# Row maxima read two banks at a time from one pair buffer, in a four-layer attention kernel

## What is computed

```python
def mla_attend(q_nope, q_rope, k_nope, k_rope, v):
    def attend(qn, qr):
        s = (jnp.einsum('bqhd,bkhd->bhqk', qn, k_nope) + jnp.einsum('bqhr,bkr->bhqk', qr, k_rope)) * scale
        p = jax.nn.softmax(s, axis=-1)
        return jnp.einsum('bhqk,bkhd->bqhd', p.astype(v.dtype), v)
...
def gqa_dense(q, k, v, sink=None):
    def attend(qb):
        s = jnp.einsum('bqhgd,bkhd->bhgqk', qb, k) * scale
        p = jax.nn.softmax(s, axis=-1)
        return jnp.einsum('bhgqk,bkhd->bqhgd', p.astype(v.dtype), v)
```

## Time and profile before

| | |
|---|---|
| median of 3 runs | 3619.41 us (3611.78 to 3621.05) |
| the profiled execution | 3618.99 us, its span 3617.2 us |
| PE, DVE, ACT, POOL busy | 3456.4, 2400.3, 2155.9, 1272.3 us |
| granted TensorE clock, mean | 0.989 |
| attention stretches (first to last p_f) | 401 to 925 (MLA), 1337 to 1804 (GQA), 2199 to 2524 (SWA), 2984 to 3493 us (MLA) |

### The profile page before, as it was taken

The page is one execution under the profiler, slowest core; times in us unless marked ns, Lnnn a source line. Parts: engine busy times, 40 slices in busy tenths (PEclk is TensorE's granted clock), DMA queues, the critical chain, the costliest instruction groups (busy, mean ns, idle before and its releaser), DMA issues. The chain is left out here.

```text
span 3617.2 us, 82216 instructions
## 1 busy us (share of the span) xinstructions
PE 3456.4 (96%) x33644; PEld 2060.7 (57%) x33644; DVE 2400.3 (66%) x3920; ACT 2155.9 (60%) x2859; POOL 1272.3 (35%) x1315
## 2 busy tenths in 40 slices
PE   6999999999999989999999998999999999999998
PEld 3554566666555556666645556666455446666654
DVE  6426688888466639999846517887553458888854
ACT  5424687887434438888823226887343338888861
POOL 0000255555230016666612003666120005555542
PEclk9999999999999999999999999999999999999999
DMA  6127523332112443333111335442112482222211
GB/s 256 52 86 218 158 69 78 82 82 65 68 36 59 130 122 74 82 75 74 43 73 52 96 115 131 109 113 69 69 46 69 134 224 56 56 56 60 53 50 59
DMA packets 373333, 325.50 MB, mean 90 GB/s; under 512 B 246272, under 2 KB 294080, under 8 KB 371424
## 3 DMA queue, kind: packets, MB, share of 16 engines
q1 hardware_dynamic: 372960, 320.24, 32.5%
HBM read 228.94 MB, written 91.23 MB: 89 GB/s over the span
## 5 line engine op out<-in xcount | busy, mean ns | idle before, releaser
L2421 POOL TENSOR_TENSOR p_lo<-p_f,p_hi 128x512 f16<-128x512 f32 (+2 forms) x768 | 836.3, 1089 | 725.2 <-DVE p_lo L2357 402.2
L2233 PE MATMUL bank<-q_slots,k_slots 96*128 96x512 f16 (+7 forms) x3968 | 1047.0, 365 | 30.3 <-PEq L1436 16.2
L798 PE MATMUL bank<-H_hilo,w_hilo 128*128 128x512 f16 (+1 forms) x5760 | 1044.7, 344 | 13.9 <-DVE w_hilo L1048 9.3
L2052 DVE TENSOR_REDUCE max_parts<-bank 128x1 f32<-128x512 f32 (+2 forms) x1536 | 959.9, 646 | 111.0 <-PE bank L1996 97.1
L2309 ACT ACTIVATE p_f<-bank 128x1024 f32<-128x1024 f32 (+2 forms) x768 | 743.5, 968 | 260.5 <-PE bank L2233 246.4
L798 PEld LDWEIGHTS bank<-H_hilo,w_hilo 128*128 128x128 f16 x5760 | 563.4, 98 | 495.0 <-DVE w_hilo L1048 10.3
L2316 ACT ACTIVATE p_hi<-bank 128x1024 f16<-128x1024 f32 (+2 forms) x768 | 743.6, 968 | 0.0
L2357 DVE TENSOR_TENSOR p_lo<-p_f,p_hi 128x512 f16<-128x512 f32 (+2 forms) x768 | 578.6, 753 | 155.4 <-ACT p_hi L2316 149.2
L1996 PE MATMUL bank<-k_slots,q_slots 96*128 96x512 f16 (+4 forms) x1536 | 561.8, 368 | 23.4 <-DVE max_parts L2052 13.1
L2233 PEld LDWEIGHTS bank<-q_slots,k_slots 96*128 96x128 f16 (+2 forms) x3968 | 345.0, 98 | 294.1 <-issue 49.4
L1012 ACT ACTIVATE z_ring<-bank 128x512 f32<-128x512 f32 (+1 forms) x192 | 87.5, 528 | 429.4 <-PE bank L798 416.1
(11 more groups left out here) (205 smaller groups left out, 4004.0 us busy)
## 6 DMA issues: line engine op xcount, KB each, us to landing
ada_w<-in_w_ada SPq DMA_DIRECT2D x48, 768.0 KB, 6.4
gate<-z_ring SPq DMA_DIRECT2D x32, 640.0 KB, 3.3
gate_rows<-gate SPq DMA_DIRECT2D x32, 640.0 KB, 4.0
q_slots<-q_mla SPq DMA_DIRECT2D x64, 240.0 KB, 3.3
k_mla<-H_hilo SPq DMA_DIRECT2D x64, 224.0 KB, 3.2
k_slots<-k_mla SPq DMA_DIRECT2D x64, 224.0 KB, 4.6
cq_hilo<-v_scratch SPq DMA_DIRECT2D x64, 224.0 KB, 4.2
v_lo_hi_one<-v_scratch SPq DMA_DIRECT2D x64, 224.0 KB, 4.2
```

The lines of the kernel that those rows point to most:

```text
L798: ins = pe.matmul(dst, lhs(a, k), rhs(b, k), start=(k == 0 and n == 0), stop=(k == nk - 1 and n == 2))
L2052: found = dve.tensor_reduce(mx[:, o, t, c:c + 1], mb[:, 0:nk], AX.X, ALU.max)
L2233: scored = pe.matmul(dst, lhs, rhs, start=(m == 0), stop=(m == len(ops) - 1), skip_group_check=swa)
L2421: pool.tensor_tensor(pl[:, g % 4, cols // 2:cols], p32[:, g % 3, cols // 2:cols], ph[:, g % 4, cols // 2:cols], ALU.subtract).then_inc(s_p ...
```

## The change

Two neighbouring entries of maxima become one: PE writes them into the two halves of bank pair 2, one DVE instruction reduces both (in MLA and GQA to two columns of `mx`; in SWA, where a pair is the two parts of one query tile, 896 or 768 columns to one). There is one such pair buffer. All other entries (turn, out, ada) share one bank, half of bank pair 3. `wait_bank` waits for the entry before of the same kind, paired or not. The lists give one pair per step. Both products of a pair stand behind the first score block, `ada` behind the last, `out` behind PV; DVE takes the pair first, `ada` and `out` last. The core of the diff:

```diff
-        SB, MB = [bank[0], bank[1]], [bank[2][:, 0], bank[2][:, 1], bank[3][:, 1]]
+        SB, MB = [bank[0], bank[1]], [bank[2][:, 0], bank[2][:, 1]]
         OB = bank[3][:, 0]
-        R = len(MB)
+        PAIR, ONE = bank[2], bank[3][:, 1]
...
+            return [("max", u, n // 2, blocks[n:n + 2]) for n in range(0, len(blocks), 2)]
...
-        out_step = [{4: 1, 5: 2}, {8: 0}] if swa else [{5: 1, 6: 2}, {11: 0}]
+        out_step = [{5: 1, 6: 2}, {8: 0}] if swa else [{7: 1, 8: 2}, {11: 0}]
...
         if swa:
-            own = [b_[5:7] + c_[:1], b_[7:] + c_[1:], [turn(1)], [turn(2)], [], [], [], [], []]
-            ahead = [[], [], [], a_[:2], a_[2:4], a_[4:6], a_[6:] + b_[:1], b_[1:3] + mod, [turn(0)] + b_[3:5]]
+            own = [b_[1:2], b_[2:3], b_[3:4], [turn(1)] + c_, [turn(2)], [], [], [], []]
+            ahead = [[]] * 4 + [a_[0:1], a_[1:2], a_[2:3], a_[3:4] + mod, [turn(0)] + b_[0:1]]
         else:
-            own = [b_[6:9], b_[9:11] + c_[:1], b_[11:] + c_[1:], [turn(1)], [turn(2)]] + [[]] * 8
-            ahead = [[]] * 4 + [a_[:2], a_[2:4], a_[4:6], a_[6:8], a_[8:10], a_[10:], b_[:3], mod + b_[3:4],
-                                [turn(0)] + b_[4:6]]
+            own = [b_[1:2], b_[2:3], b_[3:4], b_[4:5], b_[5:6], [turn(1)] + c_, [turn(2)]] + [[]] * 6
+            ahead = [[]] * 6 + [a_[0:1], a_[1:2], a_[2:3], a_[3:4], a_[4:5] + mod, a_[5:6], [turn(0)] + b_[0:1]]
...
+            if stream[b][n][1][0] == "max":
+                return PAIR
+            return MB[0] if isinstance(i, int) and i < 0 else ONE
...
-            m = place[b, n]
+            m = ring.index((b, n))
+            paired = stream[b][n][1][0] == "max"
             while True:
-                m -= R
+                m -= 1
...
-                if ring[m] is not None and wait_taken(pe, i, *ring[m]):
+                kb, kn = ring[m]
+                if (stream[kb][kn][1][0] == "max") == paired and wait_taken(pe, i, kb, kn):
                     return
...
-            found = dve.tensor_reduce(mx[:, o, t, c:c + 1], mb[:, 0:nk], AX.X, ALU.max)
+            nk = blocks[1][2]
+            if swa and u < 2:
+                found = dve.tensor_reduce(mx[:, o, n2:n2 + 1], mb[:].rearrange("p b n -> p (b n)")[:, 0:PAST + nk],
+                                          AX.X, ALU.max)
+            else:
+                found = dve.tensor_reduce(mx[:, o, 2 * n2:2 * n2 + 2], mb[:, :, 0:nk], AX.X, ALU.max)
```

More of the change, by code:

```diff
@@ L1747, in maxima_of @@
             q0, nq = units[u]
-            found = []
-            for t in range(nq // P):
-                if u == 2:
-                    found.append(("max", u, t, 0, PAST + LAT, CTX, []))
-                elif not swa:
-                    found += [("max", u, t, c, c * 512, 512, []) for c in range(3)]
-                else:
+            tiles = range(nq // P)
+            if u == 2:
+                blocks = [(t, PAST + LAT, CTX, []) for t in tiles]
+            elif not swa:
+                blocks = [(t, c * 512, 512, []) for t in tiles for c in range(3)]
+            else:
+                blocks = []
+                for t in tiles:
                     i = q0 // P + t
@@ L1809, in entry_bank, with of_kind @@
         def entry_bank(i, b, n):
-            if isinstance(i, int) and i < 0:
-                return MB[sum(d for d, e in stream[b][:n]) % 2]
-            return MB[place[b, n] % R]
+            if stream[b][n][1][0] == "max":
+                return PAIR
+            return MB[0] if isinstance(i, int) and i < 0 else ONE
+        def of_kind(b, found, *kinds):
+            return [n for n in found if stream[b][n][1][0] in kinds]
         P2 = 2 * NS
@@ L1905, in wait_bank @@
                 earlier = [m for m in range(n) if stream[b][m][0] == 1]
-                for m in earlier[-2::-2]:
+                for m in earlier[::-1]:
                     if wait_taken(pe, i, b, m):
@@ L2043, in take_entry @@
                 return
-            _, u, t, c, k0, nk, masks = e
+            _, u, n2, blocks = e
             o = turn_order[u]
@@ L2107, in attention @@
         before = [n for n, (d, e) in enumerate(stream[1]) if d == 1]
-        at_tile = [3, 3, 4, 5, 5, 6, 7, 7, 8, 8, 9, 9, 10, 10, 10, 10, 10] if swa else [3 + k * 2 // 5 for k in range(NE)]
+        at_tile = [4, 5, 6, 7, 7, 9, 10] if swa else [3, 4, 5, 6, 7, 7, 8, 9, 10] if ada else [3, 4, 5, 6, 7, 8, 9, 10]
         make_values(dict(n=len(before), at_tile=lambda k: at_tile[k], load_v=lambda sp: load_v(sp, 0, 0, 0),
@@ L2240, in body @@
                                 if n == 0:
-                                    for k in todo[:1]:
+                                    for k in of_kind(b, todo, "turn", "max"):
                                         emit_entry(pe, i, b, k)
                             scored.then_inc(s_sc.h, 1)
-                            for k in todo[1:2]:
+                            for k in of_kind(b, todo, "ada"):
                                 emit_entry(pe, i, b, k)
@@ L2248, in body @@
                         if p < P2:
-                            for k in todo[2:]:
+                            for k in of_kind(b, todo, "out"):
                                 emit_entry(pe, i, b, k)
@@ L2358, in body @@
                                               ALU.subtract).then_inc(s_pl.h, 1)
-                        for k in found[1:2]:
-                            take_entry(dve, i, b, k)
                         inverse(i, p, first)
-                        for k in found[2:]:
+                        for k in of_kind(b, found, "ada", "out"):
                             take_entry(dve, i, b, k)
```

31 lines of the change are left out of this document (16 added, 15 removed).

## The result

The changed kernel takes 3650.45 us (median of 4 runs, 3645.95 to 3653.42) beside 3618.6 us of the kernel before (median of 4): a ratio of 1.009, with a 95% interval of 1.0073 to 1.0107. Its profiled execution took 3650.79 us, with a span of 3649.0. The forecast was 3635 in a range of 3602 to 3664, so direction and range held, but the step of 32 us is twice the 16 us forecast.

What follows compares the result with a forecast made beforehand. The PE was taken to bound the kernel, busy 3456.4 us, 96% of the span. MLA +13, GQA +6, SWA -1 and -2 before the stretches gave +16 us on 3618.99: 3635 us, range 3602 to 3664.

Steps and rivals of the forecast that it cites:

- part 1: DVE's one read of two banks: 1.22 us per pair, freeing 46 us of DVE time, nothing at the end.
- part 4: Odd heads, step 11 to 12: turn(0) waits for the gate emptying the shared bank, 1.03 us MLA, 1.33 GQA, seven times a layer.
- part 3: Turns one step behind their maxima wait for neg_max: turn(0) 0.31 us MLA, 0.65 GQA; turn(1) 0.45 GQA, 0.55 SWA.
- GQA's sum: GQA stretch: 18.0 us pair-of-heads waits, 9.3 gate, 3 start, 6 late DVE; 36 against 30 before, +6 us.
- MLA's sum: Two MLA stretches: new waits 9.7 us a layer, 19.4 for both, start 3, less 9 of before: +13 us.
- start 3, less 9 of before: MLA sum's remaining terms: 3 us at the start added, the PE's earlier loss of 9 us in both stretches subtracted.
- SWA's sum: SWA stretch: 23 us of new waits plus start and small 4, against 28 before: -1 us; ada products spare even-head turn(0).
- Outside: Before each attention stretch one read less hangs at the end and half the PE's waits go: -2 us.
- (A): GQA and SWA stops go, new waits covered, MLA stays: 3569 us, about 3590 if half the waits bite; chance 0.15.
- (B): It balances: GQA and SWA gain 10 to 15 us each, MLA's out(0) wait is there: 3608 to 3625; chance 0.17.
- (C): Single pair buffer holds PE in ordinary steps, pair 1.36 us or p_lo stretched: 3670 us; chance 0.18 together with (D).
- (D): The instruction reading two banks gains nothing over two reads, same as (C); chance 0.18 together with (C).

Runs made afterwards that it cites:

- e1_out0_early: Changed kernel with unit 0's output transposes in MLA and GQA issued in step 10 of the odd head instead of step 11: 3656.61 us, ratio 1.0112.
- e1b_out_ada: As e1_out0_early, with the modulation products of the MLA and GQA heads also moved from step 10 to step 9: 3647.49 us, ratio 1.0083.
- e2_turn_later: Changed kernel with pairs issued one step earlier, so turns stand two steps behind their last maxima instead of one: 3643.52 us, ratio 1.0072.
- e5_ada_first: Changed kernel with the DVE's copy of the modulation rows issued ahead of the reciprocal instead of behind it: 3643.92 us, ratio 1.0076.
- e6_swa_out_steps: Changed kernel with SWA's output transposes of units 1 and 2 put back from steps 5 and 6 to 4 and 5: 3669.96 us, ratio 1.0146.

## Why the prediction was right, and where it was short

**The pair read** (part 1): 1.222 us for 1.22, and 46 us of the DVE for nothing. Right.

**The gate wait** (part 4): forecast 1.03 us in MLA and 1.33 in GQA, measured 0.98 and 1.31, 7 times in each. Right, with place, name and count. In e1_out0_early and e1b_out_ada, where the transposes stand a step earlier, it is gone.

**The turns behind neg_max** (part 3): turn(0) of MLA's even head 0.33 us for 0.31, GQA's turn(0) 0.66 for 0.65 and its turn(1) 0.445 for 0.45. SWA's turn(1) was forecast at 0.55 and took 0.99 in the even head and 0.37 in the odd one. Right in MLA and GQA; e2_turn_later takes them away. SWA's turn(0) of the odd head, forecast at 0.72 for neg_max, took 0.68, but behind the DVE's read of the modulation rows (L1899) in the same buffer: the size came out right by luck.

**GQA's sum**: +6 forecast, +5.8 measured. The pair that waits for its buffer behind unit 2's PV (step 2 to 3) costs 0.70 us in the even head, where 0.25 was forecast, and 0.16 in the odd one. A pair of heads loses 2.85 us beside the gate wait, for the 2.25 counted, so the 6 us for a late DVE were about the right size.

**MLA's sum** was mis-sized: +13 forecast, +20.1 measured (11.3 and 8.8). The two new waits come to 2 x (8 x 0.33 + 7 x 0.98) = 19.0 us, for the 19.4 forecast. The step that failed is "start 3, less 9 of before". The 9 us were a loss figure taken from idle time and hidden overlaps. The named waits in the MLA stretches of the kernel before came to 3.7 us of idle time, most of them at the start of a stretch, where they stay. One of them even grew (1.4 us before, now the 2.5 of the row above), in both stretches together by about 2 us. Four of the products that had stood ahead of each stretch now stand in it, 0.22 us each, 1.8 us for both, which the sum does not have. And the first stretch, at a clock of 1.00 before and 0.99 now, has a low piece of 3.4 us behind that longer stop, 1.7 us that no term of the sum could hold. That makes 24.5, so only some 4 of the 9 us were won back.

**SWA's sum** missed a mechanism: -1 forecast, +7.7 measured. The failed step is the sentence of part 3 that in the even head "the ada products stand between", read as cover for turn(0). They are what holds its buffer. The order showed all of it: turn(0) and the modulation products use the single buffer, the copy that frees it stands behind the reciprocal on the DVE, and the transposes before that had moved by a step, POOL's splits with them. I asked whether neg_max would be ready, and not who holds the bank that the turn writes. It costs 7 x 1.57 = 11.0 us; e5_ada_first took 7.5 us off the stretch, and without them the forecast for this layer would have been right to about a microsecond.

**Outside**: -2 forecast, -1.7 measured. This is luck, since the parts of it moved by -6.7 and +4.6 us (411.7 to 405.0 us between the first MLA stretch and GQA, 401.1 to 405.7 ahead of the first). The forecast had the PE wait less there; by the windows it idles for 119.7 us instead of 115.8. The time is shorter by the products that moved into the stretches and by fewer low-clock pieces.

**Rivals.** (A) and (B) rest on GQA gaining, which it does not. (C) and (D) needed a longer read. The merged read does cost 12 us in the stretches, but within the forecast's own count of the waits. No rival had a turn held by another user of the single buffer in SWA. The total, 32 us for 16, lies in the range with direction and most waits rightly named; the missing half is MLA's 7 us and SWA's 9.

## What to carry to other kernels

Before merging two reads, ask whether the reading engine is the bound. If another engine waits for the result, the merged read makes it later: here it cost 12 us in the attention stretches and gave back some 5 outside them, for 46 us of freed DVE time. Count the buffers first: one bank fewer in the old ring cost 71 us, since every entry waits for the slow readers of its bank. For each writer of a shared buffer, name who held it last, which instruction frees it, and what stands ahead of that instruction in its queue. And move one entry at a time with that table at hand: two of the repairs that moved an entry (e1, e6) only put it onto its next neighbour.

## What the runs showed of the hardware

A stop of the PE can cost more than its length. In SWA of the changed kernel stops of 1.41 us idle left the granted clock at 1.00 (the stretch's row above). In e6_swa_out_steps stops of 1.85 us idle at the same place were each followed by some 3.4 us at 0.50, and the 3 us of longer waits became 14.7 us of longer stretch. With the stops gone the clock was back at 1.00. The length of a stop does not decide it alone. The stop of 2.45 us idle near the start of each MLA stretch of the changed kernel ends at 476.34 in the first and at 3075.43 in the second. Behind the first the clock is at 0.50 for 3.4 us, behind the second it stays at 1.00:

```profile
477.00:478.00 1.00, 1.00 (x3) 0.29 (x2) 1.00 (x1) 0.00 (x0) 0.97 (x2) 0.50 0.00 0
```

```profile
3075.00:3079.00 4.00, 3.57 (x38) 2.03 (x39) 3.63 (x5) 2.22 (x3) 2.40 (x4) 1.00 0.00 0
```

Outside the attention stretches the clock moves a kernel's time by several us without an edit aiming at it: in the projections between GQA and SWA the mean clock lay between 0.97 and 0.99 and the time between 393.1 and 402.9 us. So a gain of under 10 us in this kernel is read from its stretch, with the clock and the PE's idle time beside it, and not from the total alone.
